# A two-layer encoder trunk on one core: half the tiles of the first two adaLN vectors go to TensorE as one-column matmuls

## The reference, cut to what matters

```
cond = silu(c)
mod = (cond @ ada_w[layer] + ada_b[layer]).reshape(B_, N_MOD, D)      # 1024 x 9216 weights per layer
sh1, sc1, g1, sh2, sc2, g2, sh3, sc3, g3 = [mod[:, i] for i in range(N_MOD)]
h = rmsnorm(x, norm_g[layer, 0]) * (1 + sc1) + sh1
x = x + 0.5 * g1 * swiglu(h, ff_w13[layer, 0], ff_w2[layer, 0])
...                                                                   # mixer, second feed-forward, second layer
```

## Time and profile before

| | us |
|---|---|
| median of 3 executions (1052.34, 1050.06, 1066.15) | 1052.34 |
| span of the profiled execution; the page gives no other time of its own | 1049.6 |
| TensorE busy with matmuls | 967.8 (92%) |
| VectorE busy | 737.1 (70%) |
| ScalarE busy | 433.3 (41%) |
| first matmul of the first feed-forward starts | 42.81 |

### The profile page before, as it was taken

How to read it: one execution, slowest core, us unless ns; L and a number is a source line. 1 busy time by engine, 2 the same in 40 slices (tenths; PEclk the granted TensorE clock), 3 DMA queues, 4 the chain that set the end, 5 groups by cost and what they waited for, 6 DMA issues and landing times.

```text
span 1049.6 us, 15172 instructions
## 1 busy us (share of the span) xinstructions
PE 967.8 (92%) x6272; PEld 870.5 (83%) x6272; DVE 737.1 (70%) x799; ACT 433.3 (41%) x529; POOL 123.1 (12%) x182
## 2 busy tenths in 40 slices
PE   1599999998969898999999989999999879999997
PEld 1499999986757566999999979999998779999996
DVE  4888787857887636887778578978784675454543
ACT  1343434444436434443434344343443445434341
POOL 1111111002541102111110021111110010000000
PEclk9999999998989998999999989999999889999999
DMA  9989898867533015899787666989794225555621
GB/s 340 373 303 328 300 319 284 305 172 261 204 120 121 1 41 203 277 330 343 275 318 267 212 217 232 340 295 325 277 343 159 81 81 191 191 192 170 213 69 61
DMA packets 147141, 239.59 MB, mean 228 GB/s; under 512 B 16128, under 2 KB 108160, under 8 KB 146944
## 3 DMA queue, kind: packets, MB, share of 16 engines
q1 hardware_dynamic: 126480, 166.81, 47.9%
q0 software_dynamic: 19440, 71.31, 17.7%
q10 hardware_dynamic: 1152, 0.49, 0.2%
HBM read 237.54 MB, written 1.05 MB: 227 GB/s over the span
## 4 chain that ended last, share of the span: by engine, by line
PE 83%; DVE 10%; ACT 2%; issue 2%; POOL 1%; DMA 1%; POOLq 0%; ACTq 0%; SPq 0%; DVEq 0%
PE ps L1107 55%; PE ps L1149 7%; PE ps L1150 7%; PE ps L1153 7%; DVE x L786 1%; DVE lo L694 1%; DVE xn L782 1%; PE ps L1272 1%; PE ps L1162 1%; DVE acc L740 1%; PE ps L1169 1%; PE ps L1275 1%; DMA x<-in_x 1%; POOL rstd L364 1%; DVE xn L740 1%
## 5 line engine op out<-in xcount | busy, mean ns | idle before, releaser
L1107 PE MATMUL ps<-hT_hi,hi 128*128 128x256 f32 x1408 | 405.2, 288 | 4.4 <-DVE hT_lo L803 4.4
L1107 PE MATMUL ps<-hT_lo,hi 128*128 128x256 f32 x1408 | 401.8, 285 | 0.0
L1107 PE MATMUL ps<-hT_hi,lo 128*128 128x256 f32 x1408 | 401.5, 285 | 0.0
L694 DVE TENSOR_TENSOR lo<-raw,hi 128x2048 fp32r<-128x2048 f32 (+1 forms) x110 | 244.2, 2220 | 121.4 <-ACT hi L440 121.2
L1107 PEld LDWEIGHTS ps<-hT_hi,hi 128*128 128x128 f32 x1408 | 273.5, 194 | 9.4 <-issue 7.0
L1107 PEld LDWEIGHTS ps<-hT_lo,hi 128*128 128x128 f32 x1408 | 273.7, 194 | 3.5 <-issue 1.2
L440 ACT ACTIVATE hi<-raw 128x2048 fp32r<-128x2048 f32 (+1 forms) x106 | 200.6, 1892 | 179.5 <-PE ps L1107 162.1
L1107 PEld LDWEIGHTS ps<-hT_hi,lo 128*128 128x128 f32 x1408 | 273.5, 194 | 0.0
L1149 PE MATMUL ps<-hi,u_hi 128*128 128x512 f32 x344 | 135.3, 393 | 2.8 <-DVE u_lo L714 2.7
L1150 PE MATMUL ps<-lo,u_hi 128*128 128x512 f32 x344 | 135.1, 393 | 0.0
L347 POOL DMA_DIRECT2D ada<-in_ada_w x132 | 71.6, 543 | 438.9 <-DVE acc L740 159.8
(11 more groups left out here) (128 smaller groups left out, 853.0 us busy)
## 6 DMA issues: line engine op xcount, KB each, us to landing
raw<-in_ff_w SPq DMA_DIRECT2D x264, 512.0 KB, 7.0
ada<-in_ada_w POOLq DMA_DIRECT2D x132, 512.0 KB, 7.2
raw<-in_w_in SPq DMA_DIRECT2D x24, 512.0 KB, 5.1
arena<-in_ada_w SPq DMA_DIRECT2D x4, 1024.0 KB, 19.1
raw<-in_w_out SPq DMA_DIRECT2D x8, 512.0 KB, 4.3
raw<-in_ada_w SPq DMA_DIRECT2D x2, 1024.0 KB, 15.4
arena<-in_b_rpb SPq DMA_DIRECT2D x16, 128.0 KB, 4.5
x<-in_x SPq DMA_DIRECT2D x2, 512.0 KB, 7.4
```

The costliest lines, as they stand in the source:

```text
L694: ins = V.tensor_tensor(lo, src, hi.bitcast(F32), ALU.subtract)
L1107: ins = mm(out, a, b, start=first and m == 0, stop=last and m == len(pairs) - 1, skip_group_check=shared)
```

## The change

Vectors 0 and 1 are divided. VectorE keeps tiles 0, 2, 4, 6 of vector 0 and 0, 2, 4, 5 of vector 1. TensorE takes 1, 3, 5, 7 and 1, 3, 6, 7: for each tile it runs 8 calls, call k with a 128 x 128 block of the tile as weights and `cond[:, j]` as a moving operand of one column, accumulating into column k of a PSUM bank. VectorE's accumulator is added by 8 more such calls with a column of ones. With that the vector stands finished in 8 columns of PSUM: the transposes of `mod_sum` and the reductions of line 746 are gone for these two vectors, and `mod_column` adds the bias in one operation. VectorE's tiles 0 and 2 of vector 0 move ahead of `norm_scale(0)`. SyncE's wait after vector 0 becomes a wait for both engines. GpSimd's ring for vector 2 now begins when VectorE has done tile 2 of vector 1 (and TensorE tile 1 of vector 0), and counts of `ada_used` and `mod_red` are renumbered everywhere.

```diff
+PE_TILES = ((1, 3, 5, 7), (1, 3, 6, 7))
+DVE_TILES = tuple(tuple(j for j in range(KT) if j not in PE_TILES[g]) for g in range(2))
+def ada_count(g, j):                     # VectorE tiles done, up to tile j of vector g
+def pe_ada_count(g, j):                  # TensorE tiles done, up to tile j of vector g
...
-            sp.wait_ge(ada_used, KT)
+            sp.wait_ge(ada_used, ada_count(0, KT - 1))
+            sp.wait_ge(ada_mm, pe_ada_count(0, KT - 1))
...
-                        pool.wait_ge(ada_used, n - ADA_RING + 1)
+                        if g == 2 and j < ADA_RING:
+                            pool.wait_ge(ada_used, ada_count(1, 3 + j))
+                            pool.wait_ge(ada_mm, pe_ada_count(0, j))
+                        else:
+                            pool.wait_ge(ada_used, ada_count(g if j >= ADA_RING else g - 1, (j - ADA_RING) % KT))
...
+            def mod_column(g):
+                dve.wait_ge(mod_ps, g + 1)
+                V.tensor_tensor(modc[:, g:g + 1, :], ps[:, MOD_BANK + g:MOD_BANK + g + 1, 0:KT], adab[:, g:g + 1, :],
+                                ALU.add).then_inc(mod_done, 1)
...
-            norm_scale(0)
             dve.wait_ge(cond_done, 17)
-            for g in range(2):
-                for j in range(KT):
-                    ada_tile(g, j)
-                    if g == 1 and j == 3:
-                        dve.wait_ge(adab_in, 16)
-                        mod_out(0)
+            for j in DVE_TILES[0][:2]:
+                ada_tile(0, j)
+            norm_scale(0)
+            for j in DVE_TILES[0][2:]:
+                ada_tile(0, j)
+            for j in DVE_TILES[1]:
+                ada_tile(1, j)
+            dve.wait_ge(adab_in, 16)
+            mod_column(0)
             split_lo(0)
-            mod_out(1)
+            mod_column(1)
...
+            def mod_columns(g):
+                def add(w, c, first=False, last=False):
+                    for k in range(KT):
+                        ins = mm(ps[:, MOD_BANK + g, k:k + 1], w[:, k * P:(k + 1) * P], c, start=first and k == 0,
+                                 stop=last, skip_group_check=True)
+                    return ins
+                for j in PE_TILES[g]:
+                    if g == 1 and j == PE_TILES[g][-2]:
+                        pe.wait_ge(ada_used, ada_count(g, KT - 1))
+                        add(acc_of(g), ones[:, 0:1])
+                    ins = add(ada_weights(pe, g, j), cond[:, j:j + 1], first=j == PE_TILES[g][0],
+                              last=g == 1 and j == PE_TILES[g][-1])
+                    ins.then_inc(mod_ps if (g, j) == (1, PE_TILES[1][-1]) else ada_mm, 1)
+                if g == 0:
+                    pe.wait_ge(ada_used, ada_count(g, KT - 1))
+                    add(acc_of(g), ones[:, 0:1], last=True).then_inc(mod_ps, 1)
...
             norm(0)
-            mod_sum(0)
-            pe.wait_ge(mod_red, 1)
-            mod_sum(1)
+            pe.wait_ge(cond_done, 17)
+            for g in range(2):
+                mod_columns(g)
             ffn(0)
```

More of the change, by code:

```diff
@@ L70, in norm_bank @@
     return ([0, 1, 2, 3], [6, 7, 0, 1], [0, 1, 4, 5], [6, 7, 0, 1], [5, 0, 1, 4], [4, 5, 0, 1])[s][j // 2]
+def ada_count(g, j):
+    if g < 2:
+        return sum(map(len, DVE_TILES[:g])) + sum(i <= j for i in DVE_TILES[g])
+    return sum(map(len, DVE_TILES)) + KT * (g - 2) + j + 1
+def pe_ada_count(g, j):
+    return sum(map(len, PE_TILES[:g])) + sum(i <= j for i in PE_TILES[g])
 def pair_bank(f, p):
@@ L187, in build_program @@
         uhi_done, ulo_done = sem("uhi_done"), sem("ulo_done")
-        ada_used, mod_ps, mod_red, mod_done = sem("ada_used"), sem("mod_ps"), sem("mod_red"), sem("mod_done")
+        ada_used, ada_mm = sem("ada_used"), sem("ada_mm")
+        mod_ps, mod_red, mod_done = sem("mod_ps"), sem("mod_red"), sem("mod_done")
         diag_done, gate_ps, gate_ready = sem("diag_done"), sem("gate_ps"), sem("gate_ready")
@@ L225, in unit_src, with ada_weights @@
             return raw13[:, n % 4, 0:size], [t[:, n % 2, 0:size] for t in (hi13, lo13)]
+        def ada_weights(engine, g, j):
+            n = KT * g + j
+            if ADA_RING <= n < 2 * KT:
+                m = (n - ADA_RING) // 2
+                engine.wait_ge(first_in[m], 16)
+                return first_ada[m][:, n % 2, :]
+            engine.wait_ge(ada_in[j % ADA_RING], 16 * (1 if n < ADA_RING else n // ADA_RING - 2))
+            return ada[:, j % ADA_RING, :]
         block = ctx.enter_context(nc.Block())
@@ L717, in ada_tile @@
             def ada_tile(g, j):
[L719 to L728, removed]
+                w = ada_weights(dve, g, j)
                 dst = acc_of(g)
@@ L738, in ada_tile @@
                 else:
-                    dve.wait_ge(ada_used, n)
+                    dve.wait_ge(ada_used, ada_count(g, j) - 1)
                     V.scalar_tensor_tensor(dst, w, cond[:, j:j + 1], dst, ALU.mult, ALU.add
@@ L747, in mod_out @@
                                 AX.X, ALU.add).then_inc(mod_red, 1)
-                dve.wait_ge(mod_red, g + 1)
+                dve.wait_ge(mod_red, g - 1)
                 V.tensor_tensor(modc[:, g:g + 1, :], mraw[:, :, :], adab[:, g:g + 1, :], ALU.add
                                 ).then_inc(mod_done, 1)
+            def mod_column(g):
+                dve.wait_ge(mod_ps, g + 1)
+                V.tensor_tensor(modc[:, g:g + 1, :], ps[:, MOD_BANK + g:MOD_BANK + g + 1, 0:KT], adab[:, g:g + 1, :],
+                                ALU.add).then_inc(mod_done, 1)
             def diag(g, k, scale, dst=diag_buf):
@@ L874, in _ @@
             V.memset(ones[:, :], 1.0).then_inc(setup_done, 1)
+            dve.wait_ge(cond_done, 17)
+            for j in DVE_TILES[0][:2]:
+                ada_tile(0, j)
             norm_scale(0)
-            dve.wait_ge(cond_done, 17)
-            for g in range(2):
-                for j in range(KT):
-                    ada_tile(g, j)
-                    if g == 1 and j == 3:
-                        dve.wait_ge(adab_in, 16)
-                        mod_out(0)
+            for j in DVE_TILES[0][2:]:
[4 more added lines that the diff above has]
+            mod_column(0)
             split_lo(0)
-            mod_out(1)
+            mod_column(1)
             dve.wait_ge(small_in, 16 * 7)
@@ L1157, in mod_sum @@
             def mod_sum(g, bank=MOD_BANK):
-                pe.wait_ge(ada_used, KT * (g + 1))
+                pe.wait_ge(ada_used, ada_count(g, KT - 1))
                 for j in range(KT):
@@ L1176, in ffn @@
                     if f < 3 and p >= 3 and p % 2 == 1:
-                        pe.wait_ge(mod_red, FFN_MODS[f] + (p - 1) // 2)
+                        pe.wait_ge(mod_red, FFN_MODS[f] - 2 + (p - 1) // 2)
                     if f == 2 and p == 8:
@@ L1372, in _ @@
             norm(3)
-            pe.wait_ge(mod_red, 13)
+            pe.wait_ge(mod_red, 11)
             ffn(2)
```

## The result

| | median us | executions | lowest to highest |
|---|---|---|---|
| before | 1052.88 | 4 | 1050.06 to 1066.15 |
| changed | 1076.33 | 4 (1077.76, 1061.41, 1074.90, 1077.96) | 1061.41 to 1077.96 |

The ratio of changed to before is 1.0167, with a 95% interval of 1.012 to 1.0215; it leaves out executions in a slow state, and in the changed kernel that leaves two of the four, which lie 13 us apart. The forecast was 1065 us and a range of 1047 to 1069. The direction is as forecast and the size is not: the profiled execution has a span of 1075.2 us, 25.6 us more than before, where 12.5 were forecast.

What follows compares the result with a forecast made beforehand. The start was taken to end with vector 1, then TensorE binds. 19.5 + 160 x 0.21 = 53.1 us puts the scale at 53.6, 12.5 us later; 1052.3 + 12.5 = 1064.8, rounded to 1065 us, range 1047 to 1069.

Steps and rivals of the forecast that it cites:

- Where TensorE begins: At the start, the new calls begin at 19.5 us, after 16 transposes of x that wait for VectorE's later scalings.
- What it does: On TensorE at the start, 10 groups of 8 float32 calls add 160 pairs of weight load and one-column matmul.
- What a pair costs: In the new TensorE calls, the load of 128 columns sets each pair: 0.21 us at half clock, 0.104 at full.
- Which clock: TensorE runs at half speed through the whole start; one-column matmuls were taken not to raise the clock.
- The sum: TensorE's calls end at 53.1 us, the first norm's scale at 53.6 instead of 41.11, 12.5 us later.
- the three rivals: Clock rises, 1049.4 us (0.35); cheap pairs, transfers set the end, 1046.8 (0.08); each load waits, 1084.5 (0.06).
- the first: Rival at the start: the clock rises under the one-column calls, the scale at 39.8 us, 1049.4 us in all; chance 0.35.
- The edits costed at nothing: At the start, VectorE's first-piece subtraction, SyncE's further wait and GpSimd's earlier vector 2 tiles are covered by TensorE's work.
- the bound of 38.3: GpSimd's earlier 2 MB, 5.2 us of transfers, delay the last two tiles' landing from 33.1 to at most 38.3 us.
- the first part: What bounds the kernel: the start ends when vector 1 is ready, and TensorE-bound work after it shifts one for one.

Runs made afterwards that it cites:

- the wide kernels: The first wide kernel and the wide start, changed kernels with a moving operand of 64 columns; the first gave 1049.34 to 1078.59 us, the second 1046.43 us.
- the filled pair of kernels: Kernel before and changed kernel, each with 12 float32 identity products in TensorE's wait in the mixer: 1047.01 and 1059.53 us.
- the changed one again: The changed kernel with no edit, in six more executions: 1060.09 to 1078.28 us, ratio to before 1.0101; the profiled execution took 1065.31 us.
- the delayed kernel: Kernel before plus nine more VectorE operations ahead of the reduction of vector 1, nothing of the change: 1060.81 to 1077.67 us.
- the first wide kernel: Changed kernel with the moving operand 64 columns wide, mixer wait not filled: 1049.34, 1065.42 to 1066.83 three times, 1077.84 and 1078.59 us.
- the first two wide kernels: The first wide kernel (six executions, 1049.34 to 1078.59 us) and the wide start (12 executions, 1046.43 us).
- the wide start: Changed kernel with 64 columns, mixer wait filled, VectorE tiles 0 and 1 first, vector 2's ring held until tile 6 of vector 1: 1046.43 us.
- the one with all waits at the norms filled: The wide start plus identity products around the transposes of norms 1 to 5 and ahead of the first feed-forward: 1041.71 us.
- the one with its last wait filled: The one with all waits at the norms filled, plus nine identity products in TensorE's wait for the last two adaLN tiles: 1037.75 us.

## Why the prediction was wrong

*Where TensorE begins* held: the first call at 19.15 us, forecast 19.5. *What it does* held: 160 pairs. *What a pair costs* held: 0.212 us measured, 0.21 taken. The Trainium skill ("TensorE: Matmul & The Clock Gate", section on LDWEIGHTS) gives a load as its columns over 1.2 GHz, an estimate of 107 ns; it names no clock, and "whatever the gate does" is the prediction's reading of it. The 0.111 us of the wide kernels at full clock agree within 4%; the 0.212 us at half clock do not. *Which clock* held in all three profiles with one column: 34 us of weight loads back to back did not raise it, and in the first of them it rose at 58.5 us, 3.2 us after the feed-forward's own matmuls had begun. *The sum* held: 53.60 us against 53.6, and 12.5 us as the price of the change in the filled pair of kernels. None of the three rivals came about; what the first describes, a clock that rises under the pairs, appeared in the profiles with 64 columns. One slip in it changed nothing: 20 pairs at 0.213 us from 19.5 end at 23.8 us, not 23.9.

*The edits costed at nothing* held for VectorE and SyncE. The last two tiles landed at 34.5 us in the changed kernel (issued at 19.0, landing 15.5 us later), later than 33.1 and inside the bound of 38.3, and under TensorE's work. That GpSimd's earlier issues delayed them fits the wide kernels, 36.1 us with these issues and 33.8 without.

The step that failed is in the first part: "whatever moves its start moves the end of the kernel one for one. Nothing later is touched". Nothing later is changed, but something later is not fixed. The rows that this rested on show TensorE busy from 60 to 230 us, in the first feed-forward, and were carried over to the mixer behind it, whose fall of the clock at 344.2 us stood in the earlier trace rows. The time from the scale of the second norm to that of the third was 163.9 us in one profile and 182.8 in the other, and both kernels have both, as long as the wait is not filled: the changed one by its traces, the one before by its times. The median of four then came from the upper group, 1076.33 us, 11.5 above the sum: 12.5 us were the change and some 13 the long stay at half clock, a term that the prediction put at nothing. The range failed with it: it was built from prices of the change alone, around a median. The times shown before held the warning, 1066.15 beside 1050.06 and 1052.34, and I passed over it with "two of them are within 2.8 us". A range that takes this one execution in three as it is would have reached to about 1065 + 13 = 1078 us, and held the result.

What stays open: why an execution recovers before the heads or not. The traces show only that in the 3.30 us from the fall on TensorE was busy for 3.22 and 3.30 us in the two that recovered (the kernel before, the changed one again) and for 2.55, 2.47 and 2.48 us in the three that did not (the changed, the delayed and the first wide kernel), and that at half clock the heads themselves, with TensorE busy almost without a gap, did not bring it back for 41 us. That small differences in timing decide it is a guess that no run tests. Open too is whether the change makes the long stay more likely: kernels with a later start had it in 13 of 22 executions (four of ten, four of six, and five of six with 64 columns, whose start was only 1.1 us later), the kernel before in 19 of 62. Also open is the split of both kernels' lower group into two (1047 to 1048 and 1052 to 1054 before).

## What to carry to other kernels

A matmul of one column costs its weight load, two of 128 columns in float32, 0.42 us a call at half clock: count the loads. A moving operand of 64 columns cost nothing beside the load, and in the profiles that have it the clock rose before or under the first pairs and stayed full until TensorE waited; by their times and mean clocks four of the 18 executions of the first two wide kernels did not, so it is no guarantee. Before forecasting a small change, look at the spread of the times shown: an execution 13 us off was a second mode of this program, and a wait of TensorE ahead of a stage that it bounds is the place to look. Filling such a wait with matmuls that nobody reads bought more here than the work that was moved.

## What the runs showed of the hardware

The clock rose during the 16 transposes of x in three of the twelve profiles: the delayed kernel, the wide start and the one with all waits at the norms filled. In the delayed kernel it is full behind them and falls with TensorE idle:

```profile
17.40:20.60 3.20, 0.26 (x3) 0.03 (x1) 2.89 (x4) 0.00 (x0) 0.00 (x0) 1.00 1.04 403
20.80:24.00 3.20, 0.00 (x0) 0.00 (x0) 2.99 (x3) 0.00 (x0) 0.00 (x0) 0.50 1.03 410
```

The column also reads 1.00 ahead of a trace's first record of the clock, so it is the second row, with its fall, that shows the rise; the record begins, at full, at 17.3 us. In the wide start the record begins at 17.1 us, ahead of the first pair; the transposes took 3.24 us, and the first 32 pairs ran at full clock from the start:

```profile
14.36 3.24 PE L1129 MATMUL ps<-ident,xn 128*128 128x128 f32 x16 [14.36 <-DVE xn L823]
17.44 3.68 PE L1200 MATMUL ps<-cond,ada 128*128 128x64 f32 x32
```

So that kernel does not show that 64 columns raise the clock, only that it stayed full under them; the first wide kernel and the one with its last wait filled do, with the rise at 20.5 and 19.4 us, under the pairs. In the other nine profiles the transposes took 3.65 us and left the clock at half, as in the kernel before. What decides between the two is open.

In the long stay, heads with float32 score matmuls of 256 columns kept TensorE busy for 40.08 of 40.90 us by the profile, and the clock stayed at half. In the second layer of the kernel before it rose at 624.1 us, behind 3.3 us filled with 17 fp32r matmuls of 256 columns. A busy share near 1 in the profile did not go with a rise here.
